# 64 more prompt tokens through fetched expert rows, begun after the last tile's selection, with four row slots

## The reference

```python
qh = (xb @ wq).reshape(PEER_BLOCK, PEER_HEADS, 2, PEER_DQ // 2)      # 8 heads, 2 halves of 128
s1 = einsum('nhd,kd->nhk', qh[:, :, 0], subkeys[0])                   # 128 keys each
s2 = einsum('nhd,kd->nhk', qh[:, :, 1], subkeys[1])
v1, i1 = top_k(s1, 16); v2, i2 = top_k(s2, 16)
cand = (v1[..., :, None] + v2[..., None, :]).reshape(..., 256)
sc, ci = top_k(cand, 16)
e = take(i1, ci // 16) * 128 + take(i2, ci % 16)                      # 128 experts of 16384 a token
g = softmax(sc)
a = gelu(einsum('nd,nhkd->nhk', xb, u[e]))
x = x + einsum('nhk,nhkd->nd', g * a, v[e])
```

## Time and profile before

| | |
|---|---|
| median of 3 runs | 2560.05 us (2559.35 to 2567.47) |
| the profiled execution | 2561.72 us, its span 2560.1 us |
| mean granted TensorE clock | 0.945 |
| PE, DVE, ACT, POOL busy | 2360, 1282, 358, 250 us |
| HBM read, written | 389 MB, 58 MB |
| a U tile, a V tile, a store to A | 512, 512, 192 KB |
| a load of H, a load of w | 768, 768 KB |

### The profile page before, as it was taken

How to read it: one execution, slowest core, us unless ns; L and a number is a source line. 1 busy time by engine, 2 the same in 40 slices (tenths; PEclk the granted TensorE clock), 3 DMA queues, 4 the chain that set the end, 5 groups by cost and what they waited for, 6 DMA issues and landing times. The chain is left out here.

```text
span 2560.1 us, 24392 instructions
## 1 busy us (share of the span) xinstructions
PE 2360.2 (92%) x9003; PEld 1606.2 (63%) x9003; DVE 1281.9 (50%) x2748; ACT 357.8 (14%) x649; POOL 249.6 (10%) x255
## 2 busy tenths in 40 slices
PE   7968999769998999999999999989899898999987
PEld 4745787538787876555566666655555454555576
DVE  2015577624521029999728998835445544500022
ACT  1001276400101021000012222210000000000011
POOL 1011000120000000000002121202222222100000
PEclk9978999875699999999999999989999998999998
DMA  3241211130211214444658988879999898755521
GB/s 115 53 90 61 89 58 42 45 121 17 87 66 52 74 53 136 138 145 136 200 165 298 331 317 327 324 262 338 333 328 337 310 341 309 272 181 184 158 80 44
DMA packets 177165, 448.88 MB, mean 175 GB/s; under 512 B 15133, under 2 KB 110005, under 8 KB 157718
## 3 DMA queue, kind: packets, MB, share of 16 engines
q1 hardware_dynamic: 151318, 298.91, 36.4%
q0 software_dynamic: 22272, 146.83, 15.0%
q10 hardware_dynamic: 3456, 1.57, 0.2%
HBM read 389.15 MB, written 58.11 MB: 175 GB/s over the span
## 5 line engine op out<-in xcount | busy, mean ns | idle before, releaser
L1623 PE MATMUL ex_ps<-work,ex_ring 128*128 128x384 f32 x2048 | 683.6, 497 | 56.5 <-DVE work L1759 45.5
L1570 PE MATMUL ex_ps<-h,ex_ring 128*128 128x384 f32 x2048 | 671.6, 488 | 4.7 <-DMA ex_ring<-in_uT 4.7
L1623 PEld LDWEIGHTS ex_ps<-work,ex_ring 128*128 128x128 f32 x2048 | 396.7, 195 | 343.4 <-issue 74.0
L1570 PEld LDWEIGHTS ex_ps<-h,ex_ring 128*128 128x128 f32 x2048 | 387.0, 191 | 263.7 <-DMA ex_ring<-in_uT 5.0
L1728 DVE CUSTOM_DVE_ANT_0 scores<-scores,gx_tokens 128x1024 f32<-128x1024 f32 x136 | 165.1, 1222 | 265.5 <-DMA scores<-in_uv,gx_index 242.3
L1510 POOL DMA_INDIRECT scores<-in_uv,gx_index x128 | 181.2, 1416 | 956.2 <-DVE gx_sum L1743 617.4
L1743 DVE SCALAR_TENSOR_TENSOR gx_sum<-scores,gx_hidden,gx_sum 128x1024 f32<-128x1024 f32 x136 | 174.8, 1285 | 4.9
L1759 DVE TENSOR_TENSOR work<-work 128x384 f32<-128x384 f32 x128 | 62.7, 553 | 203.2 <-DMA work<-scratch_w 203.2
L1641 ACT ACTIVATE ex_gelu<-ex_ps 128x384 f32<-128x384 f32 x128 | 62.7, 490 | 593.5 <-PE ex_ps L1570 593.5
L376 PE MATMUL gate_ps<-h,work 128*128 128x260 f32 x512 | 120.3, 389 | 2.9 <-DMA work<-in_w_t 2.9
L1305 PE MATMUL rt_ps_q<-h,rt_ring 128*128 128x260 f32 x512 | 113.8, 386 | 5.1 <-DVE h L152 5.1
(11 more groups left out here) (306 smaller groups left out, 2199.2 us busy)
## 6 DMA issues: line engine op xcount, KB each, us to landing
ex_ring<-in_uT SPq DMA_DIRECT2D x128, 512.0 KB, 3.9
ex_ring<-in_uv SPq DMA_DIRECT2D x128, 512.0 KB, 5.6
scratch_a<-ex_gelu SPq DMA_DIRECT2D x128, 192.0 KB, 3.9
scratch_w<-work SPq DMA_DIRECT2D x12, 2048.0 KB, 8.8
work<-scratch_a SPq DMA_DIRECT2D x32, 768.0 KB, 7.1
work<-scratch_w SPq DMA_DIRECT2D x32, 768.0 KB, 14.4
work<-in_w_t SPq DMA_DIRECT2D x37, 512.0 KB, 3.5
rt_ring<-in_w_q SPq DMA_DIRECT2D x16, 512.0 KB, 3.5
```

The source lines that it names most:

```text
L1570: last = nc.tensor.matmul(y[:, n % 4, 0:TD], u[:, n % UR, k, :], xn[:, k, 0:TD], start=(k == 0), stop=(k == DC - 1))
L1623: last = nc.tensor.matmul(y[:, m, 0:TD], ring[:, (E1 + e) % UR, m * P:(m + 1) * P], H[:, e // EG % 2, e % EG, :], start=(e == 0), stop=(e ...
```

## The change

TD becomes 320. The last whole tile (tokens 384 to 511) is fetched as before, and the 64 tokens 320 to 383 are fetched too: 64 more steps, each with two slots of each of the 64 tokens, in the way in which the sample's were spread. So there are 200 steps in three groups, 100 chunks, and the dense part has 80 groups of W, which begin at W0 = 128 - 40 = 88 (TURN = 86).

- `select_slots` is now a generator that yields 32 times for a tile of eight heads. `prepare` runs it for the last tile, for the sample (packed by `queries` as 64 rows of one head, S8: 11 yields), then for the dense tiles, and makes each one's gates at once. From step FIRST = 35 on VectorE takes a chunk at every fifth yield; then it takes what is left of PRE_CHUNKS = 25 in a row, turns the slots, and then makes one chunk for every five groups of W (16 in all), and two for each group of V.
- GpSimd fetches as soon as the last tile's indices are there; after 28 fetches it stores and loads the indices and gates of the 64 tokens and the sample.
- There are GR = 4 slots for fetched rows instead of 5.
- `expand` uses eight banks for tiles 8 to 81. ScalarE's exps and the chunks' gelus stand behind tiles computed from a table of times (EXP_AT, DOTS_AT).
- The first load of H is issued before the last tiles; its place in the scratch no longer overlaps what is in use.
- At the end each of the eight blocks takes two matmuls, for the last tile and for the 64 tokens.

```diff
-    TD = TP - P
-    ORDER = (GATHERED, SAMPLE, 0, 1, 2)
+    LAST = NT - 1
+    SPLIT = TD - (ND - 1) * P
+    Q = P - SPLIT
+    DENSE = (ND - 1,) + tuple(range(ND - 1))
+    ORDER = (LAST,) + DENSE
+    groups = [(LAST * P, P), (TD, Q), (TP, TS)]
...
-    W0 = 74
+    W0 = E1 - NG // PER_TILE
+    TURN = W0 - 2
+    WIDE = TURN - 4
...
-    GR = 5
-    STEPS = SLOT + TS
+    GR = 4
+    STEPS = first[-1]
...
+    EVERY = 5
+    FIRST = 32 + 3
+    HELD = 28
+    PRE_CHUNKS = 25
+    W_EVERY = 5
+    U_CHUNKS = PRE_CHUNKS + NG // W_EVERY
+    V_CHUNKS = 2
+    EXP_AT = {tile_at(us): i for i, us in enumerate((50, 71, 156, 251, 342))}
+    DOTS_AT = [tile_at(69 if k == 0 else 61.6 + 14.4 * k if k < 21 else 360 + 5.1 * (k - 20)) for k in range(PRE_CHUNKS)]
+    DOTS_AT += [W0 + (W_EVERY * k + W_EVERY) // PER_TILE - 1 for k in range(NG // W_EVERY)]
...
+            def fetch(s):
                 if s >= GR:
                     pool.wait_ge(s_gv, s - GR + 1)
...
+            pool.wait_ge(s_id, 1)
+            for n in range(HELD):
+                fetch(n)
+            pool.wait_ge(s_id, 3)
...
+            for n in range(HELD, STEPS):
+                fetch(n)
...
+            for _ in prepare():
+                step += 1
+                if step < FIRST:
+                    continue
+                if step == FIRST:
+                    dve.wait_ge(s_xk, NGR)
+                    dve.wait_ge(s_z, 1)
+                    dot(0)
+                elif (step - FIRST) % EVERY == 0:
+                    dot(chunk + 1)
+                    add(chunk)
+                    chunk += 1
...
+            while chunk < PRE_CHUNKS:
+                chunk_of(chunk)
+                chunk += 1
...
             for g in range(NG):
                 rows(g)
-                if g % (2 * PER_TILE) == 2 * PER_TILE - 1:
-                    dot(chunk + 1)
-                    add(chunk)
+                if g % W_EVERY == W_EVERY - 1:
+                    chunk_of(chunk)
                     chunk += 1
...
-                for _ in range(2):
-                    if chunk < NC:
-                        if chunk + 1 < NC:
-                            dot(chunk + 1)
-                        add(chunk)
-                        chunk += 1
+                for _ in range(V_CHUNKS):
+                    chunk_of(chunk)
+                    chunk += 1
```

More of the change, by code:

```diff
@@ L1283, in queries @@
                     scratch[:, n0 + DC * N:n0 + (DC + 1) * N], ps[:, 0:2, 0:HALF])
+        order = (NT - 1,) + tuple(range(NT - 1))
         block = ctx.enter_context(nc.Block())
@@ L1310, in _ @@
             pe.wait_ge(s_c, NG)
-            for t in range(TT):
-                m = P if t < NT else TS
+            for i, t in enumerate(order):
                 for g in range(NG):
-                    if t >= 1 and g % 4 == 0:
-                        pe.wait_ge(s_sc, (t - 1) * 4 + g // 4 + 1)
-                    last = nc.tensor.matmul(ps[0:m, g // 4, (g % 4) * P:(g % 4 + 1) * P], q[:, g, t * P:t * P + m],
+                    if i >= 1 and g % 4 == 0:
+                        pe.wait_ge(s_sc, (i - 1) * 4 + g // 4 + 1)
+                    last = nc.tensor.matmul(ps[:, g // 4, (g % 4) * P:(g % 4 + 1) * P], q[:, g, t * P:(t + 1) * P],
                                             sk[:, g % 2, :], start=True, stop=True)
@@ L1319, in _ @@
                         last.then_inc(s_s, 1)
+            pe.wait_ge(s_sc, (NT - 1) * 4 + 1)
+            pe.wait_ge(s_q8, 2)
+            for j in range(2):
+                last = nc.tensor.matmul(ps[0:TS * PH, 0, j * P:(j + 1) * P], q8[:, j].rearrange("p h b -> p (h b)"), sk[:, j, :], start=True, stop=True)
+            last.then_inc(s_s, 1)
         @block.vector
@@ L1350, in select_slots @@
         link(nc.vector.max_index(ix[0:m, g, 8:16], v[0:m, g, 8:16], w))
[L1351 to L1354, removed]
+        yield
+    vv = v[0:m, 0:2 * nh].rearrange("p (h a) k -> p h a k", a=2)
+    link(nc.vector.tensor_tensor(cd[0:m, 0:nh], vv[:, :, 0, :].unsqueeze(3).to_broadcast([m, nh, PK, PK]),
+                                 vv[:, :, 1, :].unsqueeze(2).to_broadcast([m, nh, PK, PK]), ALU.add))
+    yield
+    for h in range(nh):
         s = cd[0:m, h].rearrange("p a b -> p (a b)")
@@ L1439, in view @@
             return v
-        TT = NT + 1
+        start = free[0]
         sel = {
@@ L1537, in _ @@
                 done = (n - W0 + 1) * PER_TILE * GT
-                if n >= W0 and done <= TD and done % WB == 0:
+                if n >= W0 and done % WB == 0:
                     b = done // WB - 1
@@ L1550, in _ @@
                 load_v(e)
+            for r in range(UR):
+                sp.wait_ge(s_as[r], 16 * (E1 // UR))
             load_hidden(1)
@@ L1627, in _ @@
             for m in range(DC):
-                nc.tensor.transpose(y[:, m, TD:TP], acc[:, 0, m * P:(m + 1) * P], c.ident[:, :]).then_inc(s_ty, 1)
+                for g in range(NGR - 1):
+                    n0, q = groups[g]
+                    last = nc.tensor.matmul(y[:, m, n0:n0 + q], acc[:, g, m * P:(m + 1) * P],
+                                            c.ident[:, :] if g == 0 else spread[q][:, :], start=True, stop=True)
+                last.then_inc(s_ty, 1)
             pe.wait_ge(s_add, 1)
             for m in range(DC):
-                last = nc.tensor.matmul(y[:, 0, m * TS:(m + 1) * TS], acc[:, 1, m * P:(m + 1) * P], spread[:, :],
+                last = nc.tensor.matmul(y[:, 0, m * TS:(m + 1) * TS], acc[:, SAMPLE, m * P:(m + 1) * P], spread[TS][:, :],
                                         start=True, stop=True)
@@ L1671, in _ @@
                         g += 1
-                    if (n - W0) % 2 == 0:
-                        dots_gelu(chunk)
-                        chunk += 1
+                while chunk < U_CHUNKS and n >= DOTS_AT[chunk]:
+                    dots_gelu(chunk)
+                    chunk += 1
             while chunk < NC:
@@ new lines, in number, with prepare @@
+            def number(out, s):
+                link(nc.vector.scalar_tensor_tensor(out=out, in0=s[:, 0].rearrange("p h k -> p (h k)"), scalar=float(P),
+                                                    in1=s[:, 1].rearrange("p h k -> p (h k)"), op0=ALU.mult, op1=ALU.add))
+            def prepare():
+                for i, t in enumerate(ORDER):
+                    yield from select_slots(nc, link, c, S[:, t], se[:, t], sel, P, PH, s_e)
+                    gates(0 if i == 0 else i + 1, se[:, t], ex[:, :, :], P, PH)
+                    if i < 2:
+                        number(fi[:, i, :], se[:, t])
+                        nc.vector.tensor_copy(gidx[:, i, :], fi[:, i, :]).then_inc(s_id, 1)
+                    if i == 0:
+                        yield from select_slots(nc, link, c, S8, se8[0:SL], sel, SL, 1, s_e)
+                        gates(1, se8[0:SL], ex8[0:SL], SL, 1)
+                        number(fs[:, :], se8[0:SL])
+                        nc.vector.tensor_copy(sidx[:, :], fs[:, :]).then_inc(s_id, 1)
@@ L1747, in _ @@
-            dot(0)
+            for g in range(1, NGR):
+                n0, q = groups[g]
+                d = hrep[:, g - 1]
+                if g < SAMPLE:
+                    nc.vector.tensor_copy(d.rearrange("p k (b j) -> p k b j", b=q), xn[:, :, n0:n0 + q].unsqueeze(
+                        3).to_broadcast([P, DC, q, P // q])).then_inc(s_rep, 1)
+                    continue
+                for k in range(DC):
+                    last = nc.vector.tensor_copy(d[:, k].rearrange("p (h b j) -> p h b j", h=PH, b=TS),
+                                                 xn[:, k, TP:N].unsqueeze(1).unsqueeze(3).to_broadcast([P, PH, TS, 2]))
+                last.then_inc(s_rep, 1)
@@ new lines, in _ @@
+            for _, q in groups[1:SAMPLE]:
+                link(nc.vector.tensor_reduce(spread[q][:, :], c.ident[:, :].rearrange("p (b j) -> p b j", b=q), X, ALU.add))
+            link(nc.vector.tensor_reduce(s8a[:, :, :], c.ident[:, :].rearrange("p (h b j) -> p h b j", h=PH, b=TS),
+                                         X, ALU.add))
+            link(nc.vector.tensor_reduce(spread[TS][:, :], s8a[:, :, :].rearrange("p h b -> p b h"), X, ALU.add))
+            chunk = step = 0
+            for _ in prepare():
+                step += 1
+                if step < FIRST:
+                    continue
+                if step == FIRST:
[6 more added lines that the diff above has]
+                    chunk += 1
@@ new lines, in chunk_of @@
+            def chunk_of(k):
+                if k < NC:
+                    if k + 1 < NC:
+                        dot(k + 1)
+                    add(k)
+            while chunk < PRE_CHUNKS:
+                chunk_of(chunk)
+                chunk += 1
+            for i, t in enumerate(DENSE):
+                m = min(P, TD - t * P)
+                dve.wait_ge(s_x, i + 1)
+                nc.vector.tensor_copy(iT[:, :, t * P:t * P + m],
```

(1 more changed line is left out.)

312 lines of the change are left out of this document (160 added, 152 removed).

## The result

The changed kernel takes 2678.31 us (median of 4 runs, 2674.87 to 2680.70) against 2560.06: a ratio of 1.045 (95% interval 1.043 to 1.048), slower by 118 us. 2746 was forecast, in a range of 2636 to 2836. The profiled execution took 2674.87 us, its span is 2673.3.

A forecast was written before the change was run, and what follows sets the result against it. With V, fetches were taken to set the pace as a round trip, not the channel's rate. V's start -15 us, V +200 and tail +1 gave +186 on 2561.7, 2748; less 1.7 for the median, 2746 us, range 2636 to 2836.

The forecast's parts named there:

- the term of V: Stage with V: 929 us where it is 729 now, so +200, although TensorE has 110 us less to do.
- Rival 2: Beside V, thin traffic: every pair lands as beside U alone, 13.3 us a round, 110 us less, 2636 us; 20%.
- VectorE up to W: Before W: first fetch at 1012, five chunks in a row of 57 us, W at 1401, 70 us lost.
- W and the way into V: W: 40 tiles at 7.0 us, 280 us, to 1681; then 18 us, V beginning at 1700, 15 us earlier than now.
- The upper bound of 7.3 us a tile: In W: VectorE's 14.8 us for five groups and a chunk, with 3.5 us for a later second landing, over 2.5 tiles.
- The round beside V: With V the dot waits for a pair's second landing: rounds of 15.2 us, 58 of them making 882 us.
- The lower bound of 13.3: Beside V: the round in us if each pair lands in 10.35 us, as one fetched beside U tiles alone.
- The queries and the tail: The sample's 16 products and four copies become one, -2.5 us; at the end eight more small matmuls, +1 us.
- Rival 1: Beside V the channel sets the pace, and landings may shrink as TensorE slows: rounds of 11.4 us, 2526 us; 8%.
- The signs: Profile after: U matmuls near 400 ns or less, 59 chunks in V 15 us apart, first dots waiting, TensorE six tenths busy.
- The rule of the Trainium skill: For fetches: 2 us plus bytes at 436 GB/s, so a pair in 6.8 us, a round of 9.8, about 2433 us.
- the ring of four: Beside V: four slots let step s be fetched only once step s - 4 is added, so dots wait for second landings.

The follow-up runs named there:

- the run with 20 chunks: The changed kernel with PRE_CHUNKS 20 instead of 25, so without the five chunks in a row ahead of W: 2657.6 us, ratio 1.038.
- the run with the add first: The changed kernel, same four slots, but beside V VectorE adds chunk k before it makes the dots of chunk k + 1: 2463.3 us, ratio 0.962.
- the edits of W: Gelu earlier in ScalarE's list (2408.0 us), then W's chunk split into adds and dots (2367.5 us), on the changed kernel with add first and 20 chunks ahead of W.

## Why the prediction was right, point by point

The direction and its mechanism held; the size was some 70 us too large (2746 against 2678). It is the term of V that was too large, by 90 us, and W was too small by 16, so the two partly cancel. Rival 2, thin traffic, which had 20%, is at 2636 nearer to the result than the forecast that had 57%.

- **VectorE up to W** held nearly to the microsecond: first fetch at 1012.8 (1012), W at 1400.1 (1401), and the run with 20 chunks showed that the gap is the five in a row. The gap itself was put at 70 us and is 46: TensorE was to be ready at about 1330 and is at 1353.9, since from 943 to 1354 it waited 17.7 us for tiles of U. VectorE set the start of W, so this changed nothing in the sum; it is why the run with 20 chunks won 47 us and not 65.
- **W and the way into V** were mis-sized: 296 us to the last matmul of U and not 280, then 19.8 and not 18; V began at 1716.2 and not at 1700, +16. The upper bound of 7.3 us a tile was too low. It added up averages and a late landing, and no dot waited for a landing in W. ScalarE's order it named without a price; what it lacked is the burst against two buffers, and the slower matmuls behind each wait.
- **The round beside V is the step that failed in size**: "I take 15.2, close to the upper", and it was 13.7. The mechanism, a dot that waits for the second landing, is in the timeline, and two runs show it from both sides, a slot more and a slot less. The second landing comes 2.9 and 3.5 us after the first in the rows below, 4.6 and 2.8 in the earlier trace rows. What was too long was the landing itself, as these rows for the fetches issued at 2036.38, 2038.54, 2048.81 and 2050.98 show (us to landing):

```profile
scores<-in_uv,work POOLq DMA_INDIRECT x1, 6.6
...
gx_rows<-in_uv,work POOLq DMA_INDIRECT x1, 7.3
...
gx_rows<-in_uv,work POOLq DMA_INDIRECT x1, 7.7
...
work<-in_uv,work POOLq DMA_INDIRECT x1, 9.0
```

  The pairs are there after 2.16 + 7.3 = 9.5 and 2.17 + 9.0 = 11.2 us. I had averaged a fast and a slow round of a stage in which the DMA share was 0.92. In a slower kernel the traffic thins out, and I said so, but took off 0.3 us for it where 1.8 was right. The median landings beside V, the kernel before first, then the changed one, show that the two rows were no accident:

```profile
scores<-in_uv,gx_index POOLq DMA_INDIRECT x75, 10.0
...
gx_rows<-in_uv,work POOLq DMA_INDIRECT x36, 7.7
```

  The other slots of the changed kernel have 6.5 to 9.3. The share is 0.82, where I had said 0.6 to 0.7. The lower bound of 13.3 was the better estimate. 57 rounds of 1.5 us are 87 us less than forecast; a last round of 4.3 us takes 11 more off, an end of 52 instead of 45 gives 8 back, as three groups were left and not two: 929 becomes 839.
- **The queries and the tail** held (-1.4 us to U's first matmul, +1.4 after V).
- **Rival 1**, the channel, is wrong for this kernel: both rows are there after 9.5 us in the faster of the two rounds above, over the 9.1 at which it turns, and the channel had room, at 281 GB/s where the same 16 engines later moved 395. Its second thought, that landings shrink as TensorE slows, was right in part. The channel is, as far as the runs show, what binds once the order is changed. The share of 0.92 alone could not tell that there was room; it took the run with the add first to see it.
- **The signs**: the first dot of each chunk waits, and 59 chunks come after V's first matmul, as said. The rounds are 13.7 us and not 15, TensorE is busy 0.71 of the stretch and not 0.6, and U's matmuls have a median of 432 ns and not 400 or less.
- **The rule of the Trainium skill** doesn't agree with the trace here either (“DMA: Bandwidth & Descriptors”, section “Anatomy of one DMA”: a fixed part of 2 us and the bytes at 436 GB/s): the first of a pair lands after 6.6 us here, in a stretch in which 281 GB/s pass in all; by the page's figures it would be an estimated 4.4. No run fetched with nothing beside it.

What I didn't see was the cheapest cure, which needs no memory. I named the ring of four as the cause, but not that the order "dots of k + 1, then adds of k" is what makes four slots equal to none ahead.

## What to carry to other kernels

Count how many transfers are on their way at the moment when an engine waits, not how many buffers there are: with a software pipeline that reads k + 1 before it releases k, a ring of two chunks prefetches nothing. Releasing first cost little here: the second add of each group of V came right behind its dots and waited 0.3 us for ScalarE's gelu, 29 times, 8 us in all. A plan that averages each engine's work is only as good as its bursts against the smallest ring between two engines. And a landing time read from one kernel is not a constant: it grew and shrank here with what else was under way.

## What was unexpected of the hardware

- The DMA share of 0.92 with 326 GB/s looked like a limit and was none: with more fetches under way the same mix reached 382 and 395 GB/s, at shares of 1.02 and 1.04. The same fetch of 1 MB took longer to land as the rate rose: medians of 6.5 to 9.3 us at 281 GB/s, 9.7 to 10.4 at 381, and 10.5 to 11.8 at 395.
- TensorE's granted clock follows its waits. 1.0 is the level of 2.4 GHz. Beside V it is 0.96 before, 0.87 after, 0.97 with the add first, and where VectorE is late it costs nothing that I can see. In W, where TensorE's pace counts, it does: the same matmuls kept TensorE busy 259 us at a clock of 0.95, 249 at 0.98 and 242 at 1.00, so 17 of the 49 us that the edits of W won there are matmuls that got faster.
- GpSimd's issue of a pair's first row takes 1.86 us and that of the second 0.94, as in the timeline of 2036.38 and 2038.54 above. The first always starts while VectorE's second add is under way (it ran from 2036.14 for 1.28 us); in the changed kernel 98 of the 99 issues that overlap an add took 1.86 us or more, and 99 of the 101 others 1.03 or less. It puts the second row 2.2 us behind the first. No run tests whether the add is the cause, and it is not alone: with the add first, 16 of 37 issues that overlap a dot took 1.9 us as well.
